# Weight splits four units ahead, and behind the turned features in a second pass of token blocks

## The chip, the cores and the metric

The kernel runs on one core of a Trainium2 chip. The metric is the device time of one execution in microseconds. TensorE (PE) multiplies, VectorE (DVE), ScalarE (ACT) and GpSimd (POOL) do the elementwise work, and SyncE (SP) issues the loads of weights.

## What is computed

The reference runs two transformer blocks of two layers each on x of 256 tokens by 1024 features, in fp32. Cut to what matters here:

```
for l in range(2):                       # first block
    proj = rms_norm(x) @ w_in[l]         # parts for two attentions, pooling, gates
    merged = sum(gate_i * (branch_i @ w_branch_i[l]))
    x = x + merged @ w_out[l]
    u = conv3(rms_norm(x) @ ffn_w_up[l])
    x = x + (silu(u_gate) * u_val) @ ffn_w_down[l]
for i in range(2):                       # second block
    y = stick_breaking(rms(h) @ w_in_sb) @ w_out_sb  or  dilated(rms(h) @ w_in_dil) @ w_out_dil
    h = h + rms_norm(y)
    f = square(relu(rms_norm(h) @ w_ff_in[i])) @ w_ff_out[i]
    h = h + rms_norm(f)
    h = h + (p[i] @ w_ple[i]) * sigmoid(rms_norm(h) @ w_ple_gate[i])
```

## The kernel before

**Products.** Nearly all time goes into weights of some 240 MB, read once. They are cut into 476 units of 128 partitions by (mostly) 1024 numbers: two slices of 128 input features by 512 output columns (a panel). An fp32 product is made of three in a rounded format: high by high, high by low and low by high (L1060 to L1063 with the features moving, L1069 to L1073 with the weights moving). So each unit is **split** before use: ScalarE writes `w_high` (L1444), VectorE writes `w_low`, the rest (L1890). A load fills one of four raw slots (`RAW_SLOTS`) and waits for the low part of the load four before it; a split fills one of six split slots and its ScalarE half waits until TensorE has used the unit six before it.

**The order.** `Plan` writes one list of steps. Every engine walks through this list and does its own part of each step, in the list's order, so the list is each engine's queue. `prefetch(n)` adds the splits up to unit n + `SPLIT_AHEAD` and the loads that go with them. `unit()` calls it ahead of each whole unit's product. Behind the last unit of a panel stands the panel's evacuation (`take_...`).

**Passes by token block.** The last four units of `out`, `sb_out`, `dil_out` and `ff_out` and the first four of the matrix behind them are multiplied in two passes: first for tokens 0 to 127 (block 0), then for 128 to 255 (block 1). So the norm of block 0 runs on the other engines while TensorE does block 1, and the norm of block 1 while TensorE does block 0 of the next matrix. `first_pass` writes block 0 of the last four units, `second_pass` block 1 with the steps of `between` behind given units: behind the third and the fourth stand the turns of block 0 (`turn_t`: TensorE transposes 128 by 128 pieces, L1018, ScalarE writes the high part of the feature, L1463, VectorE the low part, L1928). Then come block 1's residual or normed addition (`residual_t`, L1938; `y_add`, L2262) and `first_units`, which does the same for the first four units of the next matrix. There `second` holds what stands behind its fourth unit: for `ff_in` that is `row`, the **diagonal** of reciprocal norms (VectorE L1958, TensorE spreads it, L1149, ScalarE copies it, L1491). Behind it stands `ff_tokens`, the **relu** of panel 0: VectorE L2271, square on ScalarE L1707, and after one further unit TensorE turns the panel (L1018).

In `dil_out`, which has only four units, `first_pass` is not used: the splits of its first pass are written between the steps of attention. In `ff_out` a unit of `ple_up` stands between the last second pass and `ple_gate`.

Of the kernel before, what the change touches and what calls it, by code (L numbers as in the profile page):

```python
# [38 lines left out]
UNIT = 1024  # L39
SPLIT_SLOTS = 6  # L40
RAW_SLOTS = 4
SPLIT_AHEAD = SPLIT_SLOTS - 1
AHEAD = 1
MASKED = -1.0e30
POOL_PAD = max(POOL_WINDOWS) // 2
# [190 lines left out]
class Plan:  # L236
# [30 lines left out]
    def prefetch(self, n):  # L267
        while self.n_split <= min(n + SPLIT_AHEAD, len(self.units) - 1):
            reach = self.units[self.n_split]["load"] + RAW_SLOTS
            if self.n_split:  # L270
                reach = min(reach, self.units[self.n_split - 1]["load"] + RAW_SLOTS)
            while self.n_loaded < min(reach, len(self.loads)):
                self.add("load", self.n_loaded)
                self.n_loaded += 1
            self.add("split", self.n_split)
            self.n_split += 1
# [32 lines left out]

    def second_pass(self, units, between):  # L310
        for i, n in enumerate(units):
            self.prefetch(n)
            self.token_unit(n, 1)
            for step in between.get(i, ()):
                self.add(*step)

    def first_units(self, name, l, take, first, second):

        units = self.own_units(name, l)[:SKEWED]
        self.prefetch(units[0])  # L320
        for i, n in enumerate(units):
            self.token_unit(n, 0)
            for step in first.get(i, ()):
                self.add(*step)
        self.second_pass(units, second)
        self.panel_end[name, l, 0] = self.n_used
        take(0)
# [84 lines left out]
    def first_pass(self, name, l):  # L412

        units = self.own_units(name, l)[-SKEWED:]
        self.prefetch(units[0])
        for n in units:
            self.token_unit(n, 0)
            self.first_pass_done(n)
        return units
# [2192 lines left out]
```

How the kernel before makes its waits and increments, by code:

```python
    def wait_ge(self, sem, value):  # L663
        if self.met.get(sem.name, 0) < value:
            self.met[sem.name] = value
            self.eng.wait_ge(sem, value)
# [1 line left out]
    def step(self, instruction):  # L668
        instruction.then_inc(self.own, 1)
        self.n += 1
# [1 line left out]
    def settle(self):  # L673
        if self.n:
            self.wait_ge(self.own, self.n)
# [27 lines left out]
    def panel_done(self, q, name, l, panel):  # L703
        q.wait_ge(self.sem("w_used"), self.plan.panel_end[name, l, panel])
# [1 line left out]
    def tokens_done(self, q, name, l, panel, t):  # L706
        if t == 0 and (name, l, panel) in self.plan.tokens_end:
            q.wait_ge(self.sem("first_tokens"), self.plan.tokens_end[name, l, panel])
        else:
            self.panel_done(q, name, l, panel)
# [136 lines left out]
    def x_ready(self, q, g, half):  # L848
        if g == STAGE_MIX[0]:
            q.wait_ge(self.sem(f"x_loaded{half}"), 16)
        elif g in (1, 2, 3, 4):
            q.wait_ge(self.sem("x_added"), self.at("residual", g, half))
        elif g == STAGE_DIL:
            q.wait_ge(self.sem("x_gated"), self.at("take_gate", 0, half))
        else:
            q.wait_ge(self.sem("y_added"), self.at("y_add", g, 1, half))
# [3 lines left out]
    def sync(self, eng):  # L861
# [6 lines left out]
            kind, key = step[0], step[1:]  # L868
            if kind == "load":
                n, = key
                if n >= RAW_SLOTS:
                    q.wait_ge(sem("w_low"), self.units_of(n - RAW_SLOTS))
                at, size = self.loads[n]
                eng.dma_start(self.raw[n % RAW_SLOTS][:, 0:size],
```

## Time and profile before

| | us |
|---|---|
| median of 3 runs | 1540.28 |
| the three runs | 1540.03, 1540.28, 1543.84 |
| the profiled execution | 1539.27 |
| its span | 1537.5 |
| TensorE busy | 1493.6 |
| VectorE busy | 1045.8 |
| ScalarE busy | 841.4 |

The profile shows one execution. Its time lies 1.0 us under the median and 1.8 above its span. Busy times of TensorE come from modelled ends, so times at which matmuls start are what to go by. Where two passes meet: `out` to `ffn_up` near 214 to 246 us and 618 to 650, `sb_out` to `ff_in` near 936 to 964, `ff_out` to `ple_gate` near 1124 to 1152 and 1493 to 1520, `dil_out` to `ff_in` near 1306 to 1332.

### The profile page before, as it was taken

What the parts mean: (1) busy time and instruction counts of PE and PEld (TensorE: products, weight loads), DVE (VectorE), ACT (ScalarE), POOL (GpSimd) and SP (SyncE); (2) the same over time, 40 slices, a digit from 0 to 9 for tenths busy, and PEclk for the clock granted to TensorE, in tenths of its full rate; (3) what the DMA queues carried; (4) which work ended last, traced back from release to release, by engine and by line L of the source; (5) the groups of instructions that cost most, each with busy time, mean ns of one, the idle gap of its engine ahead of it and who ended that gap; (6) DMA issues with size and microseconds to landing.
All of it is one profiled execution on the core that took longest, in us unless ns stands there. A gap on an engine that the chain in (4) does not pass through costs nothing.

```text
span 1537.5 us, 23829 instructions
## 1 busy us (share of the span) xinstructions
PE 1493.6 (97%) x9824; PEld 1340.0 (87%) x9824; DVE 1045.8 (68%) x1545; ACT 841.4 (55%) x1237; POOL 59.1 (4%) x70
## 2 busy tenths in 40 slices
PE   6999999999999999999999999999999998999998
PEld 5998988998899989799989977998888886799886
DVE  5798677786578877687855567665467557766446
ACT  5465556565456565665643476454456446555434
POOL 1110000000021000000000001000010000100001
PEclk9999999999999999999999999999999999999999
DMA  7543355556555435555566533655656550455661
GB/s 243 161 151 119 129 169 167 186 179 205 182 167 173 130 96 165 173 170 195 173 197 212 167 96 110 208 183 192 193 161 224 181 188 29 160 176 179 205 192 69
DMA packets 72572, 255.73 MB, mean 166 GB/s; under 512 B 8336, under 2 KB 9360, under 8 KB 72464
## 3 DMA queue, kind: packets, MB, share of 16 engines
q1 hardware_dynamic: 72176, 253.78, 51.0%
q8 instruction: 77, 1.26, 0.3%
q10 hardware_dynamic: 288, 0.43, 0.1%
q14 instruction: 31, 0.25, 0.1%
HBM read 253.14 MB, written 1.05 MB: 165 GB/s over the span
## 4 chain that ended last, share of the span: by engine, by line
PE 91%; DVE 5%; ACT 2%; issue 1%; POOL 0%; DVEq 0%; ACTq 0%; POOLq 0%
PE psum L1060 14%; PE psum L1063 14%; PE psum L1062 14%; PE psum L1069 13%; PE psum L1073 13%; PE psum L1071 13%; PE psum L1018 3%; DVE w_low L1890 2%; PE psum L1212 1%; PE psum L1297 1%; PE psum L1242 1%; ACT w_high L1444 1%; DVE dil_weights L2337 1%; DVE x_low L1928 0%; PE psum L1371 0%
## 5 line engine op out<-in xcount | busy, mean ns | idle before, releaser
L1890 DVE TENSOR_TENSOR w_low<-w_raw,w_high 128x1024 fp32r<-128x1024 f32 (+1 forms) x476 | 570.3, 1212 | 267.8 <-ACT w_high L1444 266.3
L1444 ACT ACTIVATE w_high<-w_raw 128x1024 fp32r<-128x1024 f32 (+1 forms) x476 | 495.0, 1050 | 334.4 <-PE psum L1073 188.1
L1060 PE MATMUL psum<-x_high,w_high 128*128 128x256 f32 x1504 | 429.9, 286 | 0.0
L1062 PE MATMUL psum<-x_low,w_high 128*128 128x256 f32 x1504 | 425.5, 283 | 0.0
L1063 PE MATMUL psum<-x_high,w_low 128*128 128x256 f32 x1504 | 425.4, 283 | 0.0
L1060 PEld LDWEIGHTS psum<-x_high,w_high 128*128 128x128 f32 x1504 | 288.4, 192 | 5.3 <-issue 4.6
L1062 PEld LDWEIGHTS psum<-x_low,w_high 128*128 128x128 f32 x1504 | 288.5, 192 | 0.3
L1063 PEld LDWEIGHTS psum<-x_high,w_low 128*128 128x128 f32 x1504 | 288.4, 192 | 0.0
L1069 PE MATMUL psum<-w_high,ff_high 128*128 128x512 f32 x256 | 100.0, 391 | 0.0
L1071 PE MATMUL psum<-w_low,ff_high 128*128 128x512 f32 x256 | 99.6, 389 | 0.0
L1073 PE MATMUL psum<-w_high,ff_low 128*128 128x512 f32 x256 | 99.6, 389 | 0.0
L1069 PE MATMUL psum<-w_high,x_high 128*128 128x512 f32 (+2 forms) x208 | 79.5, 382 | 5.7 <-DVE w_low L1890 4.7
L1073 PE MATMUL psum<-w_high,x_low 128*128 128x512 f32 (+2 forms) x208 | 77.3, 372 | 0.0
L1071 PE MATMUL psum<-w_low,x_high 128*128 128x512 f32 (+2 forms) x208 | 77.2, 371 | 0.0
L1069 PE MATMUL psum<-w_high,x_high_next 128*128 128x512 f32 x192 | 75.7, 394 | 0.0
L1071 PE MATMUL psum<-w_low,x_high_next 128*128 128x512 f32 x192 | 74.8, 390 | 0.0
L1073 PE MATMUL psum<-w_high,x_low_next 128*128 128x512 f32 x192 | 74.8, 389 | 0.0
L1069 PE MATMUL psum<-w_high,ffn_high 128*128 128x512 f32 x176 | 68.7, 390 | 0.0
L1071 PE MATMUL psum<-w_low,ffn_high 128*128 128x512 f32 x176 | 68.5, 389 | 0.0
L1073 PE MATMUL psum<-w_high,ffn_low 128*128 128x512 f32 x176 | 68.5, 389 | 0.0
L1060 PE MATMUL psum<-x_high_next,w_high 128*128 128x256 f32 x224 | 63.5, 284 | 0.0
L1063 PE MATMUL psum<-x_high_next,w_low 128*128 128x256 f32 x224 | 63.4, 283 | 0.0
(264 smaller groups left out, 2389.5 us busy)
## 6 DMA issues: line engine op xcount, KB each, us to landing
w_raw<-in_weights SPq DMA_DIRECT2D x462, 512.0 KB, 4.1
w_raw<-in_weights SPq DMA_DIRECT2D x8, 416.0 KB, 5.7
rows<-in_second_rows SPq DMA_DIRECT2D x4, 512.0 KB, 4.8
w_raw<-in_weights SPq DMA_DIRECT2D x6, 256.0 KB, 2.6
residual<-in_x SPq DMA_DIRECT2D x2, 512.0 KB, 5.9
out<-residual SPq DMA_DIRECT2D x2, 512.0 KB, 2.7
dil_masks<-in_consts SPq DMA_DIRECT2D x1, 576.0 KB, 5.6
rows<-in_pool_w SPq DMA_DIRECT2D x2, 256.0 KB, 5.9
```

Source lines behind the costliest of these rows:

```text
L1018: return eng.transpose(out, src, ident)
L1060: eng.matmul(o, wh[:, j, cut], high[:, k, :], start=k == 0 and f % 2 == 0, stop=False, skip_group_check=True)
L1062: eng.matmul(o, wh[:, j, cut], low[:, k, :], start=False, stop=False, skip_group_check=True)
L1063: d = eng.matmul(o, wl[:, j, cut], high[:, k, :], start=False, stop=end, skip_group_check=True)
L1069: eng.matmul(o, high[:, k, cut], wh[:, j, :], start=k == 0, stop=False, skip_group_check=True)
L1071: eng.matmul(o, high[:, k, cut], wl[:, j, :], start=False, stop=False, skip_group_check=True)
L1073: d = eng.matmul(o, low[:, k, cut], wh[:, j, :], start=False, stop=end, skip_group_check=True)
L1212: d = eng.matmul(bank[4 + i][:, t * SEQ:(t + 1) * SEQ], qt[i][:, t * P:(t + 1) * P], kt[i], start=True, stop=True)
L1242: d = eng.matmul(bank[6][HD * i:HD * i + HD, 0:SEQ], val, m["probt"][i][:, kt * SEQ:(kt + 1) * SEQ], start=kt == 0, stop=kt == TT - 1, ski ...
L1297: d = eng.matmul(o, m, r, start=False, stop=True, skip_group_check=True)
L1444: act(self.unit_view(self.wh, u), raw, ACT.Copy).then_inc(sem("w_high"), 1)
L1890: tt(self.unit_view(self.wl, u), raw, self.unit_view(self.wh, u), ALU.subtract).then_inc(sem("w_low"), 1)
```

## The change

The number of units ahead goes from five to four; the six split slots stay. In a second pass the prefetch no longer stands ahead of each unit but behind the unit and its steps, and only from the third unit on. `first_pass` prefetches for its second unit, so with four ahead it reaches as far as it did.

```diff
-SPLIT_AHEAD = SPLIT_SLOTS - 1
+SPLIT_AHEAD = SPLIT_SLOTS - 2
...
     def second_pass(self, units, between):
         for i, n in enumerate(units):
-            self.prefetch(n)
             self.token_unit(n, 1)
             for step in between.get(i, ()):
                 self.add(*step)
+
+            if i >= len(units) // 2:
+                self.prefetch(n)
...
     def first_pass(self, name, l):
 
         units = self.own_units(name, l)[-SKEWED:]
-        self.prefetch(units[0])
+        self.prefetch(units[1])
```

The diff adds two lines ahead of the engines' code, so L1890 of before is L1892 of the change.

What that does to the queues, at three places. **VectorE at the start**, before (L1899: low parts of turned features; L1909: squares; L1958: the diagonal):

```order
L1890 TENSOR_TENSOR w_low<-w_raw,w_high 128x832 x4
L1890 TENSOR_TENSOR w_low<-w_raw,w_high 128x1024 x2
L1899 SCALAR_TENSOR_TENSOR x_low<-psum,cols,x_high 128x256 x4
L1909 ISA squares,stat<-residual 128x512
L1909 ISA stat 128x1
L1918 SCALAR_TENSOR_TENSOR stat<-stat 128x2
L1890 TENSOR_TENSOR w_low<-w_raw,w_high 128x1024 x3
L1958 TENSOR_SCALAR squares<-consts,stat 128x128 x2
```

and of the change:

```order
L1892 TENSOR_TENSOR w_low<-w_raw,w_high 128x832 x4
L1892 TENSOR_TENSOR w_low<-w_raw,w_high 128x1024
L1901 SCALAR_TENSOR_TENSOR x_low<-psum,cols,x_high 128x256 x4
L1911 ISA squares,stat<-residual 128x512
L1911 ISA stat 128x1
L1920 SCALAR_TENSOR_TENSOR stat<-stat 128x2
L1892 TENSOR_TENSOR w_low<-w_raw,w_high 128x1024 x3
L1960 TENSOR_SCALAR squares<-consts,stat 128x128 x2
```

One low part of weights has moved from ahead of the second L1899 to behind it, and one fewer stands ahead of the diagonal.

**VectorE in the second pass of `dil_out`**, from the normed addition of block 0 (L2262) to that of block 1, before (L2255: gains; L2245: mean):

```order
L2262 SCALAR_TENSOR_TENSOR residual<-scratch,stat,residual 128x512 x2
L1890 TENSOR_TENSOR w_low<-w_raw,w_high 128x1024 x2
L1928 SCALAR_TENSOR_TENSOR x_low_next<-psum,cols,x_high_next 128x128 x4
L1890 TENSOR_TENSOR w_low<-w_raw,w_high 128x1024
L1928 SCALAR_TENSOR_TENSOR x_low_next<-psum,cols,x_high_next 128x128 x4
L2255 TENSOR_TENSOR scratch<-psum,rows 128x512
L2245 SCALAR_TENSOR_TENSOR stat<-stat 128x1
L2255 TENSOR_TENSOR scratch<-psum,rows 128x512
L2262 SCALAR_TENSOR_TENSOR residual<-scratch,stat,residual 128x512 x2
```

and of the change:

```order
L2264 SCALAR_TENSOR_TENSOR residual<-scratch,stat,residual 128x512 x2
L1930 SCALAR_TENSOR_TENSOR x_low_next<-psum,cols,x_high_next 128x128 x4
L1892 TENSOR_TENSOR w_low<-w_raw,w_high 128x1024 x2
L1930 SCALAR_TENSOR_TENSOR x_low_next<-psum,cols,x_high_next 128x128 x4
L1892 TENSOR_TENSOR w_low<-w_raw,w_high 128x1024
L2257 TENSOR_TENSOR scratch<-psum,rows 128x512
L2247 SCALAR_TENSOR_TENSOR stat<-stat 128x1
L2257 TENSOR_TENSOR scratch<-psum,rows 128x512
L2264 SCALAR_TENSOR_TENSOR residual<-scratch,stat,residual 128x512 x2
```

Three low parts stand between the additions in both; two of them stood ahead of the first pair of features and one between the pairs, now two stand between the pairs and one behind the second. In `sb_out` the change has one at each of these last two places.

**ScalarE at the end of `ff_in`'s first four units**, in layer 1, from the squares of the turned tokens (L1481) to the first high part of features of `ff` (L1429), before (L1491: copy of the row; L1707: square behind the relu):

```order
L1481 ACTIVATE squares,stat<-residual 128x512 x2
L1444 ACTIVATE w_high<-w_raw 128x1024 x3
L1491 ACTIVATE rstd_row<-psum 128x256
L1707 ACTIVATE scratch<-scratch 128x1024
L1444 ACTIVATE w_high<-w_raw 128x1024
L1429 ACTIVATE ff_high<-psum 128x1024
```

and of the change:

```order
L1483 ACTIVATE squares,stat<-residual 128x512 x2
L1446 ACTIVATE w_high<-w_raw 128x1024 x2
L1493 ACTIVATE rstd_row<-psum 128x256
L1446 ACTIVATE w_high<-w_raw 128x1024
L1709 ACTIVATE scratch<-scratch 128x1024
L1446 ACTIVATE w_high<-w_raw 128x1024
L1431 ACTIVATE ff_high<-psum 128x1024
```

Two splits in place of three stand ahead of the row's copy, and one stands between the copy and the square; on VectorE the same one stands between the diagonal and the relu. So it is in layer 0.

## Rows read from the trace of the kernel before

**Rows 1.** The page: busy us, share of the span, instructions of each engine.

```profile
PE 1493.6 (97%) x9824; PEld 1340.0 (87%) x9824; DVE 1045.8 (68%) x1545; ACT 841.4 (55%) x1237; POOL 59.1 (4%) x70
```

**Rows 2.** TensorE's waits in the whole span: us in total, times, longest.

```profile
PE psum L1149 <- DVE squares L1958: 4.4, 4, 1.6
PE psum L1018 <- DVE x_low L1928: 4.2, 5, 1.2
```

**Rows 3.** Groups of the splits; then, in order of time, VectorE and TensorE in ffn_down.

```profile
L1890 DVE TENSOR_TENSOR w_low<-w_raw,w_high 128x1024 fp32r<-128x1024 f32 (+1 forms) x476 | 570.3, 1212 | 267.8 <-ACT w_high L1444 266.3
L1444 ACT ACTIVATE w_high<-w_raw 128x1024 fp32r<-128x1024 f32 (+1 forms) x476 | 495.0, 1050 | 334.4 <-PE psum L1073 188.1
...
359.77 2.35 DVE L1890 TENSOR_TENSOR w_low<-w_raw,w_high 128x1024 fp32r<-128x1024 f32 x2
...
368.36 0.39 PE L1069 MATMUL psum<-w_high,ffn_high 128*128 128x512 f32 x1
```

**Rows 4.** TensorE, sb_out to ff_in: start, us, operation, [idle before <- releaser].

```profile
952.67 0.66 PE L1018 MATMUL psum<-consts,residual 128*128 128x128 f32 x4
...
963.02 0.71 PE L1149 MATMUL psum<-squares,consts 128*128 128x128 f32 x4 [1.59 <-DVE squares L1958]
...
966.44 1.04 PE L1018 MATMUL psum<-consts,scratch 128*128 128x128 f32 x8
```

**Rows 5.** ScalarE in the same stretch.

```profile
946.11 1.14 ACT L1463 ACTIVATE x_high<-psum,cols 128x128 fp32r<-128x128 f32 x4 [0.46 <-PE psum L1018]
947.12 1.07 ACT L1444 ACTIVATE w_high<-w_raw 128x1024 fp32r<-128x1024 f32 x1
...
949.21 0.62 ACT L1695 ACTIVATE squares<-psum 128x512 f32<-128x512 f32 x1
...
963.76 0.39 ACT L1491 ACTIVATE rstd_row<-psum 128x256 f32<-128x256 f32 x1 [2.53 <-PE psum L1149]
964.32 1.06 ACT L1707 ACTIVATE scratch<-scratch 128x1024 f32<-128x1024 f32 x1 [0.16 <-DVE scratch L2271]
```

**Rows 6.** VectorE in the same stretch.

```profile
944.73 2.35 DVE L1890 TENSOR_TENSOR w_low<-w_raw,w_high 128x1024 fp32r<-128x1024 f32 x2
...
951.86 1.41 DVE L2262 SCALAR_TENSOR_TENSOR residual<-scratch,stat,residual 128x512 f32<-128x512 f32 x2
...
959.07 3.50 DVE L1890 TENSOR_TENSOR w_low<-w_raw,w_high 128x1024 fp32r<-128x1024 f32 x3
962.49 0.48 DVE L1958 TENSOR_SCALAR squares<-consts,stat 128x128 f32<-128x128 f32 x2
962.88 1.40 DVE L2271 TENSOR_SCALAR scratch<-psum,stat 128x512 f32<-128x512 f32 x2
```

**Rows 7.** GpSimd in the same stretch.

```profile
959.19 1.68 POOL L2449 TENSOR_TENSOR stat<-stat,minus_half 128x2 f32<-128x2 f32 x1 [0.39 <-DVE stat L1918]
```

**Rows 8.** VectorE and TensorE, out to ffn_up in layer 0.

```profile
231.22 1.27 DVE L1938 TENSOR_TENSOR residual<-residual,psum 128x512 f32<-128x512 f32 x2
...
235.12 0.66 PE L1018 MATMUL psum<-consts,scratch 128*128 128x128 f32 x4 [1.36 <-ACT scratch L1487]
```

**Rows 9.** ScalarE at the split of unit 63; a stretch: engines' busy us, PEclk, DMA, GB/s.

```profile
217.12 1.06 ACT L1444 ACTIVATE w_high<-w_raw 128x1024 fp32r<-128x1024 f32 x1 [1.84 <-DMA w_raw<-in_weights]
...
216.00:220.00 4.00, 4.00 (x20) 3.30 (x19) 2.89 (x3) 1.06 (x1) 0.00 (x0) 1.00 0.92 278
```

**Rows 10.** VectorE and TensorE at the start.

```profile
21.73 1.65 DVE L1899 SCALAR_TENSOR_TENSOR x_low<-psum,cols,x_high 128x256 fp32r<-128x256 f32 x4
...
22.74 0.42 PE L1069 MATMUL psum<-w_high,x_high 128*128 128x416 f32 x1 [0.93 <-DVE x_low L1899]
```

**Rows 11.** A stretch of dilated attention: PE, PEld, DVE, ACT, POOL busy, PEclk, DMA.

```profile
1268.00:1272.00 4.00, 1.84 (x23) 1.44 (x20) 1.74 (x5) 3.56 (x5) 0.00 (x0) 1.00 0.42 145
```

**Rows 12.** TensorE at the lower clock of the start, and its first quicker matmul.

```profile
14.11 0.72 PE L1069 MATMUL psum<-w_high,x_high 128*128 128x416 f32 x1 [4.74 <-DVE w_low L1890]
...
19.29 0.43 PE L1069 MATMUL psum<-w_high,x_high 128*128 128x416 f32 x1
```

## Prediction

> **What bounds the kernel now.** I read five views, from coarse to fine. First the page's busy times: TensorE works 1493.6 of 1537.5 us, VectorE two thirds of it and ScalarE half [rows 1]. So the end is set by TensorE, and a change to the splits can only move the 44 us in which TensorE has nothing. Second, who TensorE waits for [rows 2]: 4.4 us in four waits for the diagonal of reciprocal norms (L1958), 4.2 us in five waits for low parts of turned features (L1928). The list of its waits has no wait for a split's low part after the first one, at the start. Third, the price of a split: 1.05 us of ScalarE and 1.21 us of VectorE, each 476 times [rows 3]. Fourth, the instructions in order of time where a second pass of token blocks stands (six places), and fifth the stretches by clock and DMA.
>
> The ring of six split slots is not touched. A split still waits until the unit six before it is used, so in a long run of whole units it is released at the same moment as before and only stands elsewhere in its engine's queue. What the change moves is that queue: ScalarE and VectorE each take their work strictly as written, as the diagonal shows: its reciprocal root was there at 960.87 (959.19 + 1.68, [rows 7]), but VectorE made it at 962.49, behind three low parts of 3.50 us [rows 6], and TensorE waited 1.59 us [rows 4].
>
> **Part 1, four ahead in place of five, whole units.** Every split stands one unit later, so an evacuation that used to stand behind a split now stands ahead of it. No instruction is added or removed. Cover: the tightest whole unit I found outside the passes by token block is the fourth of ffn_down in layer 0: its low part starts at 359.77 and takes 1.22, and its first product starts at 368.36 [rows 3]: 7.4 us of slack. By the shift a split runs at the latest when its successor ran, one unit of TensorE later. That is under 3.4 us (the diagonal and one unit of ff_in fit between 963.02 and 966.44, rows 4), so 4 us are left. This I take at nothing. If the cover were gone, each late unit would cost the missing part of 2.3 us (one high and one low part, rows 3), hundreds of times.
>
> **Part 2, the start.** Six splits stand ahead of the first product, now five. In the trace the low parts of the third and fourth pair of features start at 21.73, behind the sixth split's low part, and TensorE waits 0.93 for them at 22.74 [rows 10]. Without it they start when the fifth split ends, near 20.0, and the product of the third unit starts when the second ends, 21.65: 1.1 us gained. Of the four diagonal waits (4.4 in all, rows 2) two are the 1.6 of parts 4 and 6, so the two of proj share 1.2, each behind splits. In layer 0 I take 0.35 of 0.6 as gained (TensorE arrives 1.1 us earlier too), in layer 1, with one split fewer ahead, the whole 0.6. Sum: 2.05 gained, bounds 0.6 (only layer 1) and 2.3 (1.1 + 1.2).
>
> **Part 3, the second pass before ffn_up (twice).** Before, two splits stand ahead of the first pair of turned features, one between the pairs; now none, then one, then one before the residual. TensorE's wait of 1.2 us for the first pair's low parts (the longest of the L1928 waits, rows 2) goes. But next comes the norm of block 1: it starts with the residual on VectorE at 231.22, and TensorE waits 1.36 us for its result at 235.12 [rows 8]. ScalarE now does features, split, features, split back to back (1.12, 1.05, 1.1, 1.05 from 226.0), and VectorE's low part of the last split ends near 231.5, so the residual starts 0.28 later and so does the product behind it. The 1.2 are handed on to the later wait, which grows from 1.36 to some 3.1. Price: +0.28 each, +0.55 in all; bounds -0.3 and +1.1 each (one low part less or more ahead of the residual).
>
> **Part 4, the second pass of sb_out.** Its high parts of features start at 946.11 when TensorE has turned them, before and after. Now the first split stands behind them, where the third stood (947.12), and a second split goes between the second features and the squares of block 1. These started at 949.21 [rows 5]; they start one high part later, 950.27. VectorE has the low part of that split ahead of the gains, so the residual of block 1, at 951.86, comes 1.1 later [rows 6]. TensorE asked for it at once: its turn stands at 952.67 with next to nothing before it [rows 4]. So +1.1. Further on only two low parts stand ahead of the diagonal, not three: that gives 1.1 back at 963.02. Up to there the sum is nil.
>
> **Part 5, the split between the diagonal and the relu.** This is the term that decides. At i = 3 the diagonal is written first, then the prefetch, then the relu of panel 0. Before, the relu ran straight behind the diagonal (962.88), its square on ScalarE at 964.32 [rows 5, 6], and TensorE turned the panel at 966.44 with 1.06 to spare [rows 4]. Now ScalarE may start this split only behind its copy of the row (963.76 + 0.39, rows 5), since that stands ahead in its queue. High part to 965.2, low part to 966.4, relu (1.40) to 967.8, square (1.06) to 968.9. TensorE waits from 966.44: +2.4, with nothing else in its queue ahead of the turn. Bounds: 1.2 (2.3 for high and low part less the 1.06 of slack) and 3.5.
>
> **Part 6, the second pass of dil_out.** The same, but this pass prefetches only from its third unit on, and two splits stand between the two pairs of features (there was one). Their second high part adds 1.06 and their second low part 1.2 to the queue ahead of block 1's gains, on top of what part 4 has: the residual comes 2.4 later, not 1.1. The diagonal gives 1.1 back, part 5 comes on top: 2.4 - 1.1 + 2.4 = +3.7; bounds +1.2 and +4.8 (+2.4 and +3.5 with part 4's nil for sb_out).
>
> **Part 7, ff_out to ple_gate (twice), and the rest.** Here a unit of ple_up stands between, which hides the 1.1 of part 4. What stays is the low part of features that started behind two splits' low parts (944.73 + 2.35, rows 6, the same order in sb_out), 0.25 earlier each: -0.5. The small waits of attention I leave; a few tenths may go: -0.2. **Loads**: a load waits for the low part four before it. One place is tight: before the first pass of `out` the split of unit 63 waited for its load until 217.12; DMA moved 278 GB/s in the 4 us around it [rows 9], 1.9 us for 512 KB. Now units 58 to 61 are split later and load 63 follows load 62, so it lands near 219; the residual behind it has until about 220.5. I take it as just covered.
>
> **The sum**, against the profiled execution (1539.27, span 1537.5): -2.05 (start, diagonals) + 0.55 (ffn_up) + 0 + 2.4 (sb_out) + 3.7 (dil_out) - 0.7 (rest) = +3.9, so 1543.2. The median of the runs shown is 1.0 above that execution: 1544.2. That is 0.25% slower, under the 0.3% (4.6 us) that a measurement of this kernel can tell from no change.
>
> **The rivals.** A: the split between diagonal and relu costs nothing, because it starts ahead of the row's copy or the turn has more slack than I read. The sum is 3.9 - 4.8 = -0.9: 1539.4. For it speaks that three splits used to fit there; against it the order of ScalarE's queue. B, beyond the bound: the loads of part 7 are late. If load 63 lands at 221.1 (two transfers behind each other after 62), the residual slips past the time at which TensorE turns block 0, 1.7 us in each layer: +7.3, 1547.6. It decides from a landing at 220. Against it: at 278 GB/s the second load ends 1.9 us behind the first, not 4. C, the clock: the wait before ffn_up grows to 3.1 us, longer than any after the start. In the trace the granted clock stayed 1.00 through 4 us in which TensorE was busy for 1.84 [rows 11]. At the start, at the lower level, TensorE worked from 14.11 to 19.29 at most [rows 12], so one fall costs up to 2.6: in both layers +9.1, 1549.4. D: evacuations that no longer stand behind splits shorten the small waits of attention and all of part 3 stays gained: twice 1.2, the 2.05 and 0.7 of above, and no part 5: about -5.2, 1535.1.
>
> The Trainium skill bears on C: TensorE: Matmul & The Clock Gate, section "HAM oscillation — how this bites in real kernels", holds that long enough gaps between bursts of matmuls bring the clock down to 1.2 GHz, so that the next burst starts slow. By that rule a longer single wait is worse than two short ones of the same sum, which speaks against this change at ffn_up; the trace has no gap of that length to show it.
>
> **How the numbers follow.** The forecast has 0.60, of which 0.20 lies above 4.6 us (its bounds reach +6 or so); A 0.16; B 0.12, with 0.09 above the bound; C 0.07, all above; D 0.05, faster. Slower by over 0.3%: 0.20 + 0.09 + 0.07 = 0.36; faster 0.05; within 0.59. Range: down to 1539 takes in A; up to 1548 takes in B; C and D and the tails stay out.
>
> **What would show it.** In the trace of the changed kernel: a new wait of TensorE for L1709 (ScalarE's square) of 2.4, twice; the wait before ffn_up (L1489) near 3.1 twice, and that for L1930 nearly gone; waits for the diagonal (L1960) down from 4.4 to some 1.5; new waits for the residual in front of the turns, 1.0 at sb_out and 2.4 at dil_out; no wait for a low part of weights behind the start. The forecast is wrong if the relu runs right behind the diagonal (A), if ScalarE waits for DMA past 219.5 at unit 63 (B), or if the granted clock falls anywhere but at both ends (C).

## The result, and the profile of the changed kernel

| | before | after |
|---|---|---|
| median, us | 1540.28 | 1550.62 |
| runs | 1539.94, 1540.03, 1540.28, 1542.9, 1543.84 | 1547.07, 1547.73, 1550.62, 1551.66, 1551.98 |
| mean granted clock of these runs of after | | 0.996, 0.996, 0.992, 0.992, 0.990 |
| profiled execution, us | 1539.27 | 1551.98 |
| its span | 1537.5 | 1550.2 |

The ratio is 1.0056, 95% interval 1.0038 to 1.0073: slower by 8.6 us (10.3 between the two medians), where the forecast had 3.9, and outside the range given. The slower an execution of the changed kernel, the lower its mean clock. That is the first sign of what was missed.

The waits come first, since the forecast was made of them. TensorE's waits over the whole span of the changed kernel (two lines further down in the file than before), each with total, times and longest:

```profile
PE psum L1020 <- ACT scratch L1489: 6.4, 3, 3.0
...
PE psum L1020 <- ACT scratch L1709: 4.4, 2, 2.2
PE psum L1020 <- DVE residual L2264: 3.3, 2, 2.1
...
PE psum L1151 <- DVE squares L1960: 1.4, 4, 0.5
...
PE psum L1020 <- DVE x_low L1930: 0.4, 1, 0.4
```

Against [rows 2]: the wait for the diagonal falls from 4.4 to 1.4, that for low parts of features from 4.2 to 0.4, and three others come: for the square of the relu, twice 2.2; for the normed addition (L2264), 1.3 and 2.1; and before `ffn_up`, where [rows 8] had 1.36, now 2.9 to 3.0. No wait for a low part of weights has been added. In sb_out to ff_in the chain of part 5 reads, first ScalarE, then VectorE, then TensorE (start, us, operation, idle time before and releaser):

```profile
965.42 0.39 ACT L1493 ACTIVATE rstd_row<-psum 128x256 f32<-128x256 f32 x1 [2.64 <-PE psum L1151]
965.70 1.05 ACT L1446 ACTIVATE w_high<-w_raw 128x1024 fp32r<-128x1024 f32 x1
969.36 1.06 ACT L1709 ACTIVATE scratch<-scratch 128x1024 f32<-128x1024 f32 x1 [2.61 <-DVE scratch L2273]
...
966.78 1.23 DVE L1892 TENSOR_TENSOR w_low<-w_raw,w_high 128x1024 fp32r<-128x1024 f32 x1 [2.17 <-ACT w_high L1446]
967.92 1.40 DVE L2273 TENSOR_SCALAR scratch<-psum,stat 128x512 f32<-128x512 f32 x2
...
970.47 1.84 PE L1020 MATMUL psum<-consts,scratch 128*128 128x128 f32 x8 [2.21 <-ACT scratch L1709]
```

High part, low part, relu, square, one behind the other, as worked out ahead. In the last row stands what was not: the same eight turns that took 1.04 in [rows 4] take 1.84.

Added up over the trace between the first and the last matmul, TensorE's gaps are 29.8 us before and 32.3 after, 2.5 more; the profiled execution is 12.7 longer. The page's first line answers to [rows 1]:

```profile
PE 1502.9 (97%) x9824; PEld 1348.4 (87%) x9824; DVE 1038.3 (67%) x1545; ACT 828.7 (53%) x1237; POOL 61.3 (4%) x70
```

TensorE is busy for 9.3 us more with the same 9824 instructions. It works more slowly, and that stands in PEclk, the granted clock. Stretches of the changed kernel (busy us of PE, PEld, DVE, ACT, POOL, then PEclk, DMA share, GB/s):

```profile
232.00:236.00 4.00, 1.64 (x6) 1.54 (x7) 1.36 (x3) 3.13 (x8) 0.74 (x2) 0.67 0.33 114
236.00:240.00 4.00, 4.00 (x13) 3.12 (x13) 2.39 (x9) 1.78 (x7) 0.00 (x0) 0.50 0.37 133
640.00:644.00 4.00, 4.00 (x16) 3.35 (x16) 2.26 (x5) 2.13 (x7) 0.00 (x0) 0.63 0.27 68
968.00:972.00 4.00, 1.78 (x12) 1.58 (x10) 1.86 (x4) 2.00 (x2) 0.00 (x0) 0.83 0.40 132
972.00:976.00 4.00, 4.00 (x28) 4.00 (x27) 3.28 (x4) 2.92 (x3) 0.00 (x0) 0.74 0.40 135
1274.00:1278.00 4.00, 1.85 (x21) 1.35 (x21) 1.60 (x5) 3.61 (x8) 0.00 (x0) 0.98 0.04 12
1278.00:1282.00 4.00, 2.06 (x12) 1.18 (x10) 2.06 (x6) 1.26 (x5) 0.00 (x0) 0.50 0.00 0
1282.00:1286.00 4.00, 4.00 (x24) 3.27 (x26) 3.20 (x12) 2.31 (x6) 0.00 (x0) 0.50 0.00 0
1334.00:1338.00 4.00, 4.00 (x17) 3.22 (x17) 2.47 (x9) 2.69 (x9) 0.22 (x1) 0.77 0.86 286
```

and of the kernel before, at two of these places:

```profile
232.00:236.00 4.00, 2.64 (x14) 1.97 (x13) 1.14 (x3) 3.04 (x7) 0.75 (x2) 1.00 0.34 120
968.00:972.00 4.00, 4.00 (x36) 4.00 (x35) 2.81 (x3) 2.55 (x3) 0.00 (x0) 1.00 0.64 199
```

The clock falls to its lower level of 1.2 GHz (0.50) at five places: before `ffn_up` in both layers, behind the wait for the square at sb_out, in the dilated attention, and at dil_out. In the profiled execution of before it did so only at the ends. Four of the five places hold a new or grown wait. The fifth, the attention, does not:

```profile
1277.36 2.51 PE L1337 MATMUL psum<-dil_k,dil_q 64*128 64x256 f32 x12 [1.14 <-DVE stat L2339]
1281.81 1.66 PE L1337 MATMUL psum<-dil_k,dil_q 64*128 64x128 f32 x12 [1.94 <-DVE stat L2339]
...
1308.50 0.47 PE L1071 MATMUL psum<-w_high,dil_out_high 128*128 128x512 f32 x1
```

and in the kernel before:

```profile
1271.98 1.57 PE L1335 MATMUL psum<-dil_k,dil_q 64*128 64x256 f32 x12 [1.14 <-DVE stat L2337]
1275.49 0.94 PE L1335 MATMUL psum<-dil_k,dil_q 64*128 64x128 f32 x12 [1.95 <-DVE stat L2337]
...
1299.87 0.47 PE L1069 MATMUL psum<-w_high,dil_out_high 128*128 128x512 f32 x1
```

The same waits, 1.14 and 1.94 or 1.95; but twelve products take 2.51 in place of 1.57. They stand behind the 1.14 and ahead of the 1.94, so the clock fell between these two waits, not behind the longer one. From 1271.98 to the first product of dil_out before were 27.89 us, now 31.14 (from 1277.36): 3.25 more with no wait grown.

To place the difference I compared the start of each unit's first product in the two traces. "Queue" is what waits changed, "clock" what is left where PEclk fell:

| stretch | forecast | queue | clock |
|---|---|---|---|
| before the first matmul | 0 | +0.9 | |
| start and diagonals of proj (both layers) | -2.05 | -2.4 | |
| ffn_up, layer 0 and 1 | +0.55 | +0.6 | 1.5 and 1.0 |
| sb_out to ff_in | +2.4 | +2.4 | 1.7 |
| dilated attention | 0 | 0 | 3.2 |
| dil_out to ff_in | +3.7 | +3.3 | 0.9 |
| rest | -0.7 | -0.6 | |
| sum | +3.9 | +4.2 | 8.3 |

The split between the two columns within a stretch is worked out to some 0.3 us; the experiments test it. The 0.9 of the first row is the wait for the load of constants, 7.4 before and 8.3 after. It is not the change's: in the eight other profiled executions, whatever their edit, it is 7.9 to 8.2. Without it the queue's column gives +3.3. The attention's 3.2 is not certain to be the change's either, as further runs show.

### The profile page after: what moved, and what is told of

The parts are those of the page before. It is cut to its first block, busy times and chain, and to the rows that moved or that the text cites. A ratio compares the mean times of both kernels' runs of the same rounds, so it can differ in the third digit from the quotient of the medians.

```text
span 1550.2 us, 23777 instructions
## 1 busy us (share of the span) xinstructions
PE 1502.9 (97%) x9824; PEld 1348.4 (87%) x9824; DVE 1038.3 (67%) x1545; ACT 828.7 (53%) x1237; POOL 61.3 (4%) x70
## 4 chain that ended last, share of the span: by engine, by line
PE 64%; DVE 4%; ACT 2%; DMA 1%; issue 1%; POOL 0%; SPq 0%; DVEq 0%; ACTq 0%; POOLq 0%
PE psum L1071 10%; PE psum L1073 10%; PE psum L1075 10%; PE psum L1062 9%; PE psum L1064 9%; PE psum L1065 9%; PE psum L1020 2%; DVE w_low L1892 2%; PE psum L1299 1%; DMA w_raw<-in_weights 1%; PE psum L1214 1%; PE psum L1337 1%; ACT w_high L1446 1%; DVE dil_weights L2339 1%; PE psum L1244 0%
## 5 line engine op out<-in xcount | busy, mean ns | idle before, releaser
L1892 DVE TENSOR_TENSOR w_low<-w_raw,w_high 128x1024 fp32r<-128x1024 f32 (+1 forms) x476 | 562.5, 1211 | 177.9 <-ACT w_high L1446 177.7
L1446 ACT ACTIVATE w_high<-w_raw 128x1024 fp32r<-128x1024 f32 (+1 forms) x476 | 484.5, 1050 | 200.2 <-PE psum L1075 125.1
L1631 ACT ACTIVATE scratch<-psum,cols 128x256 f32<-128x256 f32 x88 | 42.8, 564 | 62.3 <-PE psum L1065 58.8
L2181 DVE SCALAR_TENSOR_TENSOR scratch<-psum,cols,scratch 128x255 f32<-128x255 f32 x88 | 38.2, 476 | 43.4 <-ACT scratch L1631 43.4
```

Of the source, the lines that this page charges most:

```text
L1446: act(self.unit_view(self.wh, u), raw, ACT.Copy).then_inc(sem("w_high"), 1)
L1631: d = act(o[:, f, :], acc[:, f, :], ACT.Identity, scale=conv_w[:, 2 * FT + ft:2 * FT + ft + 1], bias=conv_b[:, ft:ft + 1])
L1892: tt(self.unit_view(self.wl, u), raw, self.unit_view(self.wh, u), ALU.subtract).then_inc(sem("w_low"), 1)
L2181: q.step(stt(o[:, f, 1:], u[:, f, 0:SEQ - 1], tap(0, f), o[:, f, 1:], ALU.mult, ALU.add))
```

## The experiments

Two theories. **Q**: the order of the queues alone; the time is the sum of TensorE's waits. **C**: TensorE's pauses, new ones and old ones together, also bring its clock down, and that costs as much again. A rival to both is that with only four splits ahead the splits themselves come late, and that this is what slows it. Each run had its own runs of the kernel before beside it: two sets, medians 1541.77 and 1541.74. Those of the first result had 1540.28, so the sets are best compared by their ratios.

### The two halves: four ahead alone, and the second pass alone

Four ahead alone:

```
-SPLIT_AHEAD = SPLIT_SLOTS - 1
+SPLIT_AHEAD = SPLIT_SLOTS - 2
 ...
-        self.prefetch(units[0])      # first_pass
+        self.prefetch(units[1])
```

> The first half of the change alone: splits stand four units ahead (and a first pass begins with the second of its units), while a second pass of token blocks keeps its splits ahead of the turned features, as before. Theory Q (the order of the queues alone, the clock stays at full speed): TensorE's new waits for ScalarE's square (L1709) are gone, the residual waits are as before, the diagonal waits are shorter; start and projection 2.05 us gained, some 0.8 at each ffn_up, nothing lost: about 3.6 us less than before, 1536.7 against 1540.3, ratio 0.9977. Theory C (the waits of the second pass bring TensorE's clock down, and each fall costs 1 to 3 us): no wait of the change's second pass is here, so the granted clock stays 1.00 between the ends but perhaps in the dilated attention; also near 1536.7, up to 3.2 more with a fall there. If four ahead is itself harmful (loads or splits late), TensorE waits for low parts of weights and it is slower than before.

Measured: 1537.28, ratio 0.9972 (0.9961 to 0.9982), seven runs from 1536.59 to 1540.41. The profiled one kept 1.00 between the ends. Its waits:

```profile
PE psum L1018 <- DVE x_low L1928: 3.4, 5, 0.8
...
PE psum L1149 <- DVE squares L1958: 3.2, 2, 1.6
PE psum L1018 <- ACT scratch L1487: 2.7, 2, 1.4
```

The two short diagonal waits of proj are gone and only the two of 1.6 are left; TensorE waits for no split but the first, at the start, as before. So four ahead is a gain by itself, 4.3 us by the ratio (2.6 between the two profiled executions, both at a mean clock of 0.999) against 3.6 expected, and late splits are not what slows the changed kernel.

The second pass alone, `SPLIT_AHEAD` left at five:

```
 def second_pass(self, units, between):
     for i, n in enumerate(units):
-        self.prefetch(n)
         self.token_unit(n, 1)
         for step in between.get(i, ()):
             self.add(*step)
+        if i >= len(units) // 2:
+            self.prefetch(n)
```

> The other half of the change alone: splits five units ahead as before, in a second pass of token blocks behind the turned features as in the changed kernel. If the two halves add up, this one carries all the new waits (before block 1's first turn, L1709 twice 2.2, the clock's falls) and none of the start's gain: the whole change measured 10.3 us over before and four ahead alone 4.5 under it, so some 13 to 15 us over before, near 1555. Theory Q (no clock) gives only 7 us over before, 1549. If four ahead is needed to make the new waits (they interact), it is near before.

Measured: 1558.11, ratio 1.0103 (1.0088 to 1.0117), four runs. 15.9 us slower by the ratio, above the 13 to 15 that adding up gave. Its rows at the two `ffn_up`, and the clock in and behind the two waits (PEclk stands behind the five engines):

```profile
237.96 0.66 PE L1020 MATMUL psum<-consts,scratch 128*128 128x128 f32 x4 [3.69 <-ACT scratch L1489]
...
643.21 0.66 PE L1020 MATMUL psum<-consts,scratch 128*128 128x128 f32 x4 [3.71 <-ACT scratch L1489]
```

```profile
240.00:244.00 4.00, 4.00 (x17) 3.01 (x16) 2.28 (x9) 1.63 (x5) 0.00 (x0) 0.74 0.39 131
...
640.00:644.00 4.00, 0.79 (x6) 0.75 (x7) 1.24 (x3) 3.01 (x6) 0.75 (x2) 1.00 0.54 195
644.00:648.00 4.00, 3.20 (x16) 2.22 (x15) 3.12 (x9) 2.28 (x9) 0.00 (x0) 1.00 0.36 125
```

3.69 against 2.96 in the whole change and 1.36 before. The first of the two waits brought the clock down, the second, longer by 0.02, left it at 1.00 in the same execution. With five ahead the second pass of `out` catches up with two splits at once between the pairs of features, as dil_out does in part 6. So the loss is all in this half, and the first half takes a part of it back: -4.3 + 15.9 = 11.6, the whole change has 8.6. The 3.0 between these two are in part the shorter waits with four ahead and in part the doubt of three ratios; they were not told apart.

### The split put behind the relu

The changed kernel, but the prefetch behind the fourth unit of `first_units` left out (the next whole unit then makes it):

```
-            if i >= len(units) // 2:
+            if len(units) // 2 <= i < last:      # last = 3 from first_units
                 self.prefetch(n)
```

> The changed kernel, but the split that stands between the diagonal and the relu (the fourth unit's, in sb_out and dil_out) stands behind the relu. Theory Q: the two waits of TensorE for L1709 (2.2 each, 4.4 in all) go, the residual waits stay (1.3 and 2.1); about 4.4 us less than the changed kernel, 1546.2 against 1550.6. Theory C: the same and, since the second gap behind each residual wait is gone, the granted clock no longer falls near 970 and 1333 us (1.7 and 0.8 us): 6 to 7 us less than the changed kernel, near 1544; the falls at ffn_up (two) and in the dilated attention stay. If part 5 of the prediction is wrong, the wait for L1709 stays whatever the order.

Measured: 1542.15, ratio 1.0000 (0.9991 to 1.0009), against 1.0056 of the whole change. TensorE's wait for L1709 is gone, and the stretch keeps its clock. In order of time:

```profile
966.43 1.06 ACT L1709 ACTIVATE scratch<-scratch 128x1024 f32<-128x1024 f32 x1 [0.17 <-DVE scratch L2273]
...
968.55 1.04 PE L1020 MATMUL psum<-consts,scratch 128*128 128x128 f32 x8
```

and as a stretch:

```profile
968.00:972.00 4.00, 4.00 (x36) 4.00 (x36) 3.46 (x4) 3.76 (x5) 0.00 (x0) 1.00 0.39 130
```

One split at the wrong side of one evacuation, twice in the program, cost 4.4 us of waits and, by the two ratios, 8.6 us of time (some 3 of doubt; 6.2 between the two profiled executions), against 4.4 by theory Q and 6 to 7 by theory C. The edit leaves the same split out of the pass of ffn_up too, where the wait before block 1's turn is as long as in the changed kernel (2.9). Part 5's mechanism stands: 0.17 ahead of the square in place of 2.61. The other falls were still there in the profiled execution (0.58 at 236 to 240, 0.50 at 640 to 644, 0.57 at 1328 to 1332, and 0.63 in the attention at 1274 to 1278); that was the longest of its eleven, with a mean clock of 0.992, the others had 0.992 to 0.998. That dil_out still falls is against what I expected of C there: the wait of 2.06 for the addition brings the clock down without the one for the square behind it.

### The waits filled with work

The decisive run for C. In the changed kernel TensorE does matmuls nobody uses where it waits: they write into the bank that the next turn overwrites, and nothing that TensorE waits for comes earlier by it.

```
+        def fill(count, n, out):
+            v = self.unit_view(self.wh, self.units[n])
+            q.wait_ge(sem("w_low"), n + 1)
+            for _ in range(count):
+                eng.matmul(out, v[:, PANEL:PANEL + P], v[:, 0:PANEL], start=True, stop=True, ...)
 ...
+                if t == 1 and part == 0 and g in FILL:     # FILL = {1: 10, 3: 10, 5: 4, 8: 8}
+                    acquire(b)
+                    fill(FILL[g], used, bank[b])
 ...
+                if name == "ff_in":                        # ahead of the turn of panel 0
+                    fill(FILL_PANEL, used + 1, bank[2 * s])    # FILL_PANEL = 8
```

> The changed kernel with matmuls whose results are never used, put in front of TensorE's new waits: 10 of 0.23 us before the first turn of block 1 at ffn_up in both layers, 4 there at sb_out, 8 at dil_out, and 8 before each relu panel 0 is turned. Nothing that is waited for comes earlier, so by theory Q (only the waits cost) the time is that of the changed kernel, 1550.6, or a little more. By theory C (TensorE without work loses its clock, and that costs on top of the waits) the clock stays 1.00 at ffn_up, sb_out and dil_out, which gives 1.5 + 1.0 + 1.7 + 0.8 = 5.0 us back: near 1545.6, though longer on paper; the fall in the dilated attention (3.2 us) may stay.

Measured: 1545.87, ratio 1.0023 (1.0014 to 1.0032), so 5.1 us less than the changed kernel by the ratios, with 48 matmuls more; the intervals of the two ratios leave some 3 us of doubt on that difference, so its size is known only roughly; where it comes from is read from the clock's rows. Ten runs lie from 1544.01 to 1547.59; an eleventh took 5249.27 us with a mean clock of 1.00, which no trace explains and which is not in the ratio. TensorE before the turn of `ffn_up` in order of time, and behind it stretches of the same run:

```profile
231.67 2.20 PE L1028 MATMUL psum<-w_high 128*128 128x512 f32 x9
234.52 0.66 PE L1022 MATMUL psum<-consts,scratch 128*128 128x128 f32 x4 [0.65 <-ACT scratch L1503]
```

```profile
236.00:240.00 4.00, 3.20 (x16) 2.22 (x15) 2.93 (x10) 2.66 (x8) 0.00 (x0) 1.00 0.42 133
...
972.00:976.00 4.00, 4.00 (x35) 4.00 (x35) 4.00 (x5) 2.93 (x3) 0.00 (x0) 1.00 0.55 154
1278.00:1282.00 4.00, 2.46 (x16) 2.24 (x17) 3.23 (x11) 1.95 (x4) 0.00 (x0) 0.50 0.00 0
```

The turn comes at 234.52 (234.36 without the fill), but takes 0.66 and not 1.12, and what follows runs at 1.00. The four falls at the passes are gone, and with them about what the table has for them (1.5 + 1.0 + 1.7 + 0.9 = 5.1). The one in the attention, which this run does not fill, is still there. With work there too, ahead of the first three products of scores:

```
+                if u < 3:                                # dil_scores
+                    acquire(4)
+                    fill((4, 4, 8)[u], used + 1, bank[4])
```

> The changed kernel with the unused matmuls of the earlier fill run and 16 more (4, 4 and 8) ahead of the first three products of scores in the dilated attention. Theory C: the granted clock is 1.00 from the start to the end in nearly every run, the spread closes, and the time is what the sum of the queue's waits gives: 1543.5 to 1544.5, about 1.5 less than with the first fill (1545.9), 6 less than the changed kernel. If the attention's fall has another cause than TensorE's pauses, the clock falls there as before and the time is 1545.9 or, with the fillers' own time, more.

Measured: 1545.50, ratio 1.0021 (1.0012 to 1.0030), eleven runs from 1544.51 to 1546.48.

```profile
1274.00:1278.00 4.00, 3.98 (x23) 2.77 (x23) 2.33 (x7) 1.76 (x5) 0.00 (x0) 1.00 0.00 0
1278.00:1282.00 4.00, 3.66 (x33) 2.57 (x31) 3.86 (x15) 3.28 (x9) 0.00 (x0) 1.00 0.00 0
```

The clock is 1.00 everywhere between the ends and the spread is 2.0 us, where the changed kernel had 4.9. Its time is 1.0 above what I had expected at most, though, and against the run before it nothing is gained that the ratios can show (1.0023 and 1.0021): the attention's fall is not in every run, and the fillers cost something themselves. The next run gives that cost.

### The attention's fall in the kernel before

> The kernel before with the 16 unused matmuls in the dilated attention alone. Its runs spread over 4.5 us, and the mean granted clock of a run falls with its time (0.999 at 1539.7, 0.996 at 1543.9). Theory C: the spread is the dilated attention's fall in part of the runs; with the fillers all runs are near 1540 with a clock of 0.999, so a median about 1.8 lower than before's 1541.8, ratio 0.9988. Otherwise (falls elsewhere, or other noise) the same median and spread as before.

The edit is the last one, in the kernel before. Measured: 1541.29, ratio 0.9996 (0.9987 to 1.0005), eleven runs from 1541.02 to 1542.88; the 21 runs of before beside it went from 1540.18 to 1545.37. The spread closed from 5.2 to 1.9 us, as C says, and no run was above 1543; but the median moved by 0.45 and not by 1.8. The fastest is 0.8 later: the first product of dil_out starts 0.6 later in its trace, against the products ahead of it, which is the fillers' price. So this speaks for C as the cause of the long runs, and the cure is not free. It is no proof: only 5 of the 21 runs of before are above 1543, and no long run of before was traced. What is on record is that its runs at 0.999 took 1540.2 to 1540.9, those at 0.996 or 0.995 1543.7 to 1545.4, and that this distance fits the attention's 3.2.

### The diagonal and the relu ahead, four splits ahead

> Four ahead, and in the second pass of sb_out and dil_out the first two splits stand ahead of the features as before, the diagonal and the relu stand ahead of the other two; in all other second passes as before. Theory Q: the gains of four ahead (2.05 at the start and at the projections, 0.8 at each ffn_up) and the diagonal waits of 1.6 gone in both layers: 6.8 us less than before, 1533.5, ratio 0.9956. Theory C adds nothing here if the waits are short: the granted clock stays 1.00 but perhaps in the dilated attention. Rival: the splits put behind the relu are late for the first units of ff_in, and TensorE waits for low parts of weights (L1892): then no better than the kernel with four ahead alone.

```
+SPLIT_AHEAD = SPLIT_SLOTS - 2                # and units[1] in first_pass
 def second_pass(self, units, between, last=4):
     for i, n in enumerate(units):
+        if i < last:                         # last = 2 from first_units
             self.prefetch(n)
```

Measured: 1539.69, ratio 0.9981 (0.9972 to 0.9990), eleven runs from 1537.21 to 1542.07: no better than with four ahead alone (0.9972; the two intervals overlap), where I expected 0.9956. Both diagonal waits of 1.6 are gone, but ahead of dil_in ScalarE (in order of time) and TensorE (its waits) show one that I had not foreseen:

```profile
1159.24 1.06 ACT L1445 ACTIVATE w_high<-w_raw 128x1024 fp32r<-128x1024 f32 x1 [3.16 <-DMA w_raw<-in_weights]
```

```profile
PE psum L1019 <- DVE residual L2314: 3.1, 1, 3.1
```

A load of weights came late, the split behind it too, and the residual behind that: 3.1 in place of 0.9. It is the mechanism of rival B, at another place. The execution also has a fall in the attention (0.57 at 1270 to 1274), and none of the eleven runs has a mean clock above 0.998. The rival of the expectation, splits late for ff_in, did not come; one wait of 0.3 for a low part of weights stands at 1523.55.

So the last kernel does it only where no dil_in follows, at dil_out, and fills the attention:

```
-        self.second_pass(units, second, 2)
+        self.second_pass(units, second, 2 if (name, l) == ("ff_in", 1) else 4)
```

> Four ahead with the splits of second passes where they were, in the second pass after dil_out alone the diagonal and the relu ahead of the last two splits, and the 16 unused matmuls in the dilated attention. Theory Q gives four ahead's 3.1 to 3.6 and the diagonal wait's 1.6 in that one layer; theory C adds some 0.6 to 1.8 for the clock that no longer falls in the attention. Together 1535.0, ratio 0.9957 (the kernel with four ahead alone had 0.9972, the one with both layers changed 0.9981). If the late load before dil_in, seen in the run with both layers changed, comes from the change in dil_out and not in sb_out, it is not gone and this is no better than 1537.

Measured: 1535.61, ratio 0.9956 (0.9944 to 0.9969), five runs from 1534.94 to 1536.05: the fastest kernel here, 6.8 us under the kernel before. Its waits:

```profile
PE psum L1019 <- ACT scratch L1498: 3.0, 3, 1.4
...
PE psum L1157 <- DVE squares L1969: 1.8, 2, 1.6
...
PE psum L1019 <- DVE residual L2324: 0.9, 1, 0.9
```

The late load went with the change at sb_out. That this change moves it rests on one traced execution of each kernel; by which path was not followed, and it stays open.

## Why the prediction failed, point by point

- **Part 1** (whole units cost nothing): right. The changed kernel has no wait for a low part of weights behind the start.
- **Part 2** (-2.05): the start alone gave 1.9, the two diagonals of proj the rest, -2.4 in all, just past the bound of 2.3.
- **Part 3** (+0.28 each, the wait growing to 3.1): the wait grew to 2.96 and 2.91, and the 1.2 was gained ahead of it: +0.3 each. Right as a sum of waits.
- **Parts 4 and 6** (the addition late by 1.1 and 2.4, the diagonal 1.1 early): waits of 1.3 and 2.1 measured, the diagonal 1.1 and 1.3 early.
- **Part 5** (+2.4 twice): 2.2 twice. Rival A is out; the run with the split behind the relu shows the mechanism and its price.
- **Part 7** (-0.7, the load of unit 63 near 219): -0.6, and that split started at 218.22. B did not happen in the changed kernel.
- **What failed** is the silent step of the sum: every term was counted with TensorE at 1.00 throughout, so the clock's term was nothing. In its place the two traces show 8.3 us, 5.1 of them behind the four new or grown waits and 3.2 in the attention; and work put into the four waits took 5.1 us back by the ratios, about what lies between the measured 8.6 and the forecast 3.9. Rival C named the mechanism, but was wrong in chance and place. I gave it 0.07 because the clock had stayed up through 4 us with 1.84 busy [rows 11]; that is one execution, and the changed kernel's fall lies at that very place, in a stretch with 1.85 busy. I also asked only about the wait before ffn_up, the longest. The 2.2 at sb_out, with 1.3, 0.4 and 0.5 in the 16 us ahead of it, and the single 2.05 at dil_out brought it down as well. The price per fall at the passes, 0.9 to 1.7, lies under my "up to 2.6"; the attention's 3.2 lies above it.
- **A clue that I passed by**: the runs of before shown were 1540.03, 1540.28 and 1543.84. The third lies 3.6 above the second, which is the size of one fall in the attention; no trace of such a run was taken. The 1.0 between the profiled execution and the median, which I took as a constant, is no more than the spread among runs that kept their clock (1540.18 to 1540.92 at 0.999).

Without the clock the sum was right to some 1.5 us. Three ways lead there. By the table the queue gives +3.3 on the profiled execution without the 0.9 ahead of the first matmul, against +3.9. fill_all, whose clock does not fall, lies 3.2 us over before by the ratio, and 4.8 over the middle one (1540.69) of the runs of before at 0.999; the fillers' own 0.6 or more is to be taken off both. And the changed kernel's own runs lie 0.8 us lower per 0.001 of mean clock (from 1551.98 at 0.990 to 1547.07 at 0.996), so at 0.999 they would be near 1544.6, an estimate, where the forecast was 1544.2. Some luck is in the last: the queue's sum came out 0.6 under the forecast, and the 1.0 that I had added for the median had no cause that I knew.

Two of the five places have a pattern that the prediction did not use: several short waits follow each other ahead of the fall (1.02 and 1.14 in the attention; 1.3, 0.4, 0.5 and 2.2 at sb_out). The other three do not: there the clock fell at one wait with none above 0.5 near it (2.96 and 2.91 before ffn_up, 2.05 at dil_out). What tells a wait that brings the clock down from one that does not stays open. The Trainium skill (TensorE: Matmul & The Clock Gate, section "A second HAM failure mode: psum-queue depth-cycling") tells of a kernel whose clock goes back and forth because TensorE idles briefly but often between groups of matmuls. The rows of the attention and of sb_out agree with it, and it was the section to cite beside the one on long gaps: by it the attention and the pass of sb_out were candidates, not ffn_up alone.

## What to carry to other kernels

Where an engine's queue is the order of a list, a step put behind an evacuation delays nothing only if the evacuation is the one that the bound engine asks for next; ask it of each evacuation apart. And price a wait of TensorE twice: once as itself, once with the products behind it at half clock, at every place where a wait of some us is new or grows, near others or alone. A spread of some us between executions with a mean clock that follows it is a sign that such places are there already. Unused matmuls in a wait are a quick test of it, but no free cure: in the kernel before they cost 0.6 us, and what they saved could not be told from nothing (0.9996).

## What the runs showed of the hardware

- The same waits in the same order (1.14 and 1.94 or 1.95 in the attention) went with 0.50 in the traced executions of five kernels (the changed one, the second pass alone, the split behind the relu, the first fill, and the diagonal and the relu ahead) and with 1.00 in two (before, and four ahead alone). In one execution a wait of 3.69 brought the clock down and one of 3.71 at the same step of the next layer did not. One profile does not tell that a place is safe.
- In the changed kernel no wait where it fell was longer than 2.96 us, and at dil_out and sb_out the longest were 2.05 and 2.2. I had looked for the longest wait alone.
- At 0.50 the matmuls of 128x256 start 0.21 to 0.22 us apart (972.32, 972.54, 972.75), at 1.00 0.12 (975.00, 975.12), so the same work takes 1.8 times as long:

```profile
972.32 0.41 PE L1064 MATMUL psum<-x_low,w_high 128*128 128x256 f32 x1
972.54 0.41 PE L1065 MATMUL psum<-x_high,w_low 128*128 128x256 f32 x1
972.75 0.41 PE L1062 MATMUL psum<-x_high,w_high 128*128 128x256 f32 x1
...
975.00 0.28 PE L1065 MATMUL psum<-x_high,w_low 128*128 128x256 f32 x1
975.12 0.28 PE L1062 MATMUL psum<-x_high,w_high 128*128 128x256 f32 x1
```
